# A two-layer decoder trunk on one core: query and gate tiles ahead of the value tiles, an earlier compress, work shared with ScalarE and GpSimd, and a normalisation that needs no second pass

## The reference

```python
h = jnp.einsum('btd,de->bte', x, w_in)          # 1024 -> pool, conv, q, k/v, gates, merge gates
y_a = pool_mixer(pu, ...) * silu(pz)
y_b = cb * short_conv(cc * cx, ...) * silu(cz)
kc = partial_rope(compress(k_cmp_all, ...), kc_end); vc = compress(v_cmp_all, ...)
# attention = g0 * compressed + g1 * selected blocks + g2 * sliding window; gates g = sigmoid(ng)
y_c = nsa_mixer(q, kc, vc, ks, vs, kw, vw, gates, ...) * silu(az)
merged = g_a * (y_a @ proj_a) + g_b * (y_b @ proj_b) + g_c * (y_c @ proj_c)
z = ALPHA * x + merged @ w_out
mu = mean(z); var = mean((z - mu) ** 2)
x = (z - mu) * rsqrt(var + 1e-5) * ln_g + ln_b
```

## Time and profile before

| | us |
|---|---|
| median of 3 runs | 802.36 |
| lowest, highest | 801.02, 804.2 |
| the profiled execution, its own time | 804.0 |
| its span, first to last instruction | 802.3 |
| PE busy | 770.2 (96%) |
| DVE busy | 557.0 (69%) |
| ACT busy | 400.2 (50%) |
| POOL busy | 90.5 (11%) |

### The profile page before, as it was taken

One profiled execution on the slowest core, in us unless ns is written; L12 is line 12 of the kernel. 1 busy time (PEld: TensorE's weight loads), 2 busy tenths in 40 slices (PEclk: granted clock), 3 DMA queues, 4 the chain that ended last, 5 costly groups with the idle time before them and its releaser, 6 DMA issues.

```text
span 802.3 us, 16955 instructions
## 1 busy us (share of the span) xinstructions
PE 770.2 (96%) x6354; PEld 720.4 (90%) x6354; DVE 557.0 (69%) x1038; ACT 400.2 (50%) x793; POOL 90.5 (11%) x166
## 2 busy tenths in 40 slices
PE   8999979999999999999999978799999999999995
PEld 8998778888889999999879978788988999999994
DVE  4564679997679575657465666799886876665664
ACT  5442456666555444443345442676755464444423
POOL 2333430000133100000000034200000000000000
PEclk9999999999999999999999998999999999999998
DMA  8988756533868766555348786636348356665521
GB/s 313 285 272 294 228 179 216 190 103 107 293 227 261 233 179 181 179 181 175 106 136 229 257 246 209 235 113 211 103 123 308 118 183 184 184 183 175 181 93 55
DMA packets 42331, 154.95 MB, mean 193 GB/s; under 512 B 6416, under 2 KB 7440, under 8 KB 41616
## 3 DMA queue, kind: packets, MB, share of 16 engines
q1 hardware_dynamic: 33952, 115.55, 45.8%
q0 software_dynamic: 8304, 38.37, 14.4%
HBM read 145.77 MB, written 13.34 MB: 198 GB/s over the span
## 4 chain that ended last, share of the span: by engine, by line
PE 87%; DVE 6%; DMA 2%; ACT 2%; issue 1%; SPq 0%; DVEq 0%; ACTq 0%
PE bank L664 22%; PE bank L665 22%; PE bank L666 22%; PE bank L682 3%; PE bank L882 3%; DMA ring<-weights_dram 2%; DVE w_lo L1199 2%; PE bank L826 1%; PE bank L832 1%; PE bank L837 1%; PE bank L675 1%; PE bank L1003 1%; PE bank L923 1%; PE bank L1012 1%; PE bank L862 1%
## 5 line engine op out<-in xcount | busy, mean ns | idle before, releaser
L1199 DVE TENSOR_TENSOR w_lo<-ring,w_hi 128x1024 fp32r<-128x1024 f32 x202 | 248.3, 1231 | 155.7 <-ACT w_hi L1021 151.8
L664 PE MATMUL bank<-x_hi,w_hi 128*128 128x264 f32 x1208 | 352.5, 292 | 2.2 <-DVE w_lo L1199 2.2
L666 PE MATMUL bank<-x_lo,w_hi 128*128 128x264 f32 x1208 | 344.5, 285 | 0.0
L665 PE MATMUL bank<-x_hi,w_lo 128*128 128x264 f32 x1208 | 344.4, 285 | 0.0
L1021 ACT ACTIVATE w_hi<-ring 128x1024 fp32r<-128x1024 f32 x202 | 213.3, 1057 | 68.9 <-PE bank L666 34.0
L664 PEld LDWEIGHTS bank<-x_hi,w_hi 128*128 128x128 f32 x1208 | 229.9, 190 | 6.6 <-issue 3.3
L665 PEld LDWEIGHTS bank<-x_hi,w_lo 128*128 128x128 f32 x1208 | 229.9, 190 | 0.4
L666 PEld LDWEIGHTS bank<-x_lo,w_hi 128*128 128x128 f32 x1208 | 228.8, 189 | 0.0
L664 PE MATMUL bank<-h_rounded,w_hi 128*128 128x264 f32 x352 | 102.2, 290 | 0.0
L665 PE MATMUL bank<-h_rounded,w_lo 128*128 128x264 f32 x352 | 100.2, 285 | 0.0
L1073 ACT ACTIVATE h<-bank 128x264 f32<-128x264 f32 x88 | 34.6, 393 | 99.0 <-PE bank L666 90.6
(11 more groups left out here) (253 smaller groups left out, 994.6 us busy)
## 6 DMA issues: line engine op xcount, KB each, us to landing
ring<-weights_dram SPq DMA_DIRECT2D x208, 512.0 KB, 3.7
cache_a<-kcmp_dram POOLq DMA_DIRECT2D x32, 128.0 KB, 3.8
cache_b<-vcmp_dram POOLq DMA_DIRECT2D x32, 128.0 KB, 3.5
cache_a<-ksel_dram POOLq DMA_DIRECT2D x32, 128.0 KB, 4.2
cache_b<-vsel_dram POOLq DMA_DIRECT2D x32, 128.0 KB, 2.6
cache_a<-kwin_dram POOLq DMA_DIRECT2D x2, 2048.0 KB, 11.7
cache_b<-vwin_dram POOLq DMA_DIRECT2D x2, 2048.0 KB, 8.9
kv_dram<-h POOLq DMA_DIRECT2D x2, 1584.0 KB, 6.9
```

The lines of the kernel that those rows point to most:

```text
L664: pe.matmul(out, w_high[:, k0 + k, :], high, start=(k == 0), stop=False)
L665: pe.matmul(out, w_rest[:, k0 + k, :], high, start=False, stop=False)
L666: ins = pe.matmul(out, w_high[:, k0 + k, :], rest, start=False, stop=(k == kn - 1))
L1199: dve.tensor_tensor(w_lo[:, slot % RING], ring[:, slot % RING], w_hi[:, d % HI_RING].bitcast(F32), ALU.subtract).then_inc(w_lo_ready, 1)
```

## The change

The first 25 tiles come in another order (`FIRST_TILES`): the four value tiles VS, VW stand behind Q and NG. The small steps are listed by place (`AFTER_PLACE`), and those of the compress products by layer (`COMPRESS_STEPS`): in layer two cmp_k and cmp_v stand behind places 13 and 14. The row copies of cmp_swap are shared: two larger copies on DVE and two on ACT in place of eight on DVE. q_pad goes from DVE to GpSimd, behind the loads of the selected values. The new rows of k and v are stored by two DMAs in place of one, and k_split waits for that of the keys alone.

The normalisation takes z less a shift (the mean of the channels of tile 0), sums z and its squares while the out tiles run (GpSimd adds tile by tile, ACT squares), and takes the variance as mean of squares less squared mean. Left of the matmuls by ones are five in each layer: one for the shift, two for the mean and two for the squares; the idle matmuls go.

```diff
@@ -91,19 +91,27 @@
...
-AFTER_DENSE = {
-    8: [("rope", 0)], 9: [("cmp_swap", 0)], 10: [("rope", 1), ("cmp_swap", 1)], 13: [("v_rows", 0), ("v_rows", 1)],
-    15: [("v_new_in", 0)], 16: [("rope", 2)], 17: [("cmp_k", 0)], 18: [("v_new", 0), ("rope", 3)], 19: [("cmp_sum", 0)],
-    20: [("rope", 4), ("cmp_rope", 0), ("cmp_v", 0), ("gates", 0)], 21: [("rope", 5), ("q_pad", 0)],
-    22: [("cmp_scores", 0), ("k_split", 0), ("cmp_sum", 1)], 23: [("cmp_vrows", 0), ("cmp_back", 0)],
-    24: [("q_split", 0), ("cmp_soft", 0)]}
+FIRST_TILES = [*range(KC, VS), *range(Q, NG + 1), *range(VS, Q), *range(NG + 1, 25)]
+COMPRESS_STEPS = (
+    {16: [("cmp_k", 0)], 18: [("cmp_sum", 0), ("cmp_v", 0)], 19: [("cmp_rope", 0)], 20: [("cmp_sum", 1)]},
+    {13: [("cmp_k", 0)], 14: [("cmp_v", 0)], 15: [("cmp_sum", 0)], 17: [("cmp_rope", 0)], 19: [("cmp_sum", 1)]})
+AFTER_PLACE = {
+    8: [("rope", 0)], 9: [("cmp_swap", 0)], 10: [("rope", 1)], 11: [("cmp_swap", 1)], 12: [("rope", 2)],
+    14: [("rope", 3)], 16: [("rope", 4)], 17: [("gates", 0)], 18: [("rope", 5)],
+    20: [("cmp_scores", 0)], 21: [("cmp_vrows", 0), ("cmp_back", 0)],
+    22: [("v_rows", 0), ("v_rows", 1), ("v_new_in", 0), ("k_split", 0)], 23: [("cmp_soft", 0), ("v_new", 0)], 24: [("q_split", 0)]}
+
+
+AFTER_OUT = {1: [("shift", 0)], 3: [("square", 0), ("square", 1)], 4: [("square", 2), ("square", 3)],
+             5: [("square", 4)], 6: [("square", 5)]}
...
-    for n in range(25):
-        order += [("dense", n)] + AFTER_DENSE.get(n, [])
+    for n, tile in enumerate(FIRST_TILES):
+        order += [("dense", tile)] + AFTER_PLACE.get(n, [])
+        order += COMPRESS_STEPS[l].get(n, [])
...
-        order.append(("out", i))
-        if i:
-            order.append(("mean", i - 1))
+        order += [("out", i)] + AFTER_OUT.get(i, [])
     if l == DEPTH - 1:
-        return order + [("mean", KT8 - 1), ("warm", 0), ("squares", 0), ("norm", 0)]
-    order += [("pre_k", 0), ("mean", KT8 - 1), ("pre_k", 1), ("pre_k", 2), ("squares", 0)]
-    order += [("pre_k", t) for t in range(3, KT8)] + [("pre_v", t) for t in range(KT8)]
+        return order + [("mean", 0), ("square", 6), ("square", 7), ("norm", 0)]
+    order += [("pre_k", 0), ("mean", 0), ("pre_k", 1), ("square", 6), ("square", 7)]
+    order += [("pre_k", t) for t in range(2, KT8)] + [("pre_v", t) for t in range(KT8)]
...
+                pool.memset(zf[:, 0:NB * GP * 32], 0.0).then_inc(q_pad_clear, 1)
+                pool.wait_ge(q_pad_clear, l + 1)
+                go()
...
+                for i in range(1, KT8 - 1):
+                    if i == 1:
+                        pool.wait_ge(shifted, l + 1)
+                    else:
+                        wait_emptied(pool, l, "out", i)
+                    go()
+                    pool.tensor_tensor(z_sum, z_sum if i > 1 else z[:, 0, :], z[:, i, :], ALU.add).then_inc(z_summed, 1)
+                    pool.wait_ge(squared, l * KT8 + i + 1)
+                    go()
+                    pool.tensor_tensor(h[:, 0, :], h[:, 0, :], h[:, i, :], ALU.add).then_inc(squares_summed, 1)
+                    pool.wait_ge(z_summed, l * (KT8 - 2) + i)
+                    pool.wait_ge(squares_summed, l * (KT8 - 2) + i)
...
+                    elif step == "shift":
+                        wait_emptied(pe, l, "out", 0)
+                        pe.matmul(bank[SA][:, 0:T], ones[:, :], z[:, 0, :], start=True, stop=True).then_inc(shift_sum, 1)
+                    elif step == "square":
+                        if i == KT8 - 2:
+                            pe.wait_ge(squares_summed, (l + 1) * (KT8 - 2))
+                            pe.matmul(bank[SB][:, 0:T], ones[:, :], h[:, 0, :], start=True, stop=False)
+                        elif i == KT8 - 1:
+                            pe.wait_ge(squared, (l + 1) * KT8)
+                            pe.matmul(bank[SB][:, 0:T], ones[:, :], h[:, i, :], start=False, stop=True
+                                      ).then_inc(squared_sum, 1)
...
                     elif step == "mean":
...
+                        pe.wait_ge(shift_ready, l + 1)
+                        pe.wait_ge(z_summed, l * (KT8 - 2) + KT8 - 2)
+                        pe.matmul(bank[SA][:, 0:T], ones[:, :], z_sum, start=True, stop=False)
+                        wait_emptied(pe, l, "out", KT8 - 1)
+                        pe.matmul(bank[SA][:, 0:T], ones[:, :], z[:, KT8 - 1, :], start=False, stop=True
+                                  ).then_inc(mean_ready, 1)
...
+                    elif step == "cmp_swap":
+                        own = (cache_a, cache_b)[i][:, CMP_CACHED:CMP_CACHED + CMP_OWN].rearrange(
+                            "p (s u g c) -> p u g c s", u=2, g=4, c=CT)
+                        act.wait_ge(own_landed[i], (l + 1) * 2 * 16)
+                        for j in range(2):
+                            rows = slice(j * HD, j * HD + HD)
+                            ins = act.activation(own[rows, 0, 1 - j::2, :, :], z[rows, 4 + 2 * i:6 + 2 * i, 0:SEQ].rearrange(
+                                "p g (c j s) -> p j g c s", c=CT, j=2)[:, j], ACT.Copy)
+                        ins.then_inc(cmp_swapped, 1)
...
+                    elif step == "shift":
+                        act.wait_ge(shift_sum, l + 1)
+                        act.activation(z_shift, bank[SA][:, 0:T], ACT.Copy, scale=float(KT8)).then_inc(shift_ready, 1)
+                    elif step == "square":
+                        if i < 2:
+                            act.wait_ge(shifted, l + 1)
+                        else:
+                            wait_emptied(act, l, "out", i)
+                        act.activation(h[:, i, :], z[:, i, :], ACT.Square).then_inc(squared, 1)
                     elif step == "norm":
-                        for k in range(4):
-                            act.wait_ge(centered, l * 4 + k + 1)
-                            act.activation(m[:, 2 * k:2 * k + 2, :], z[:, 2 * k:2 * k + 2, :], ACT.Square
-                                           ).then_inc(squared, 1)
-                        act.wait_ge(squared_sum, l + 1)
-                        act.activation(rstd[:, :], bank[SB][:, 0:T], ACT.Sqrt, bias=eps[:, :]).then_inc(std_ready, 1)
+                        act.wait_ge(mean_ready, l + 1)
+                        act.activation(mean_sq, bank[SA][:, 0:T], ACT.Square).then_inc(mean_squared, 1)
+                        act.wait_ge(var_ready, l + 1)
+                        act.activation(rstd[:, :], rstd[:, :], ACT.Sqrt, bias=eps[:, :]).then_inc(std_ready, 1)
...
+                    if step == "gates":
                         wait_emptied(dve, l, "dense", NG)
...
+                        for n in range(2):
+                            wait_emptied(dve, l, "dense", (KC, VC)[i] + n)
+                        for j in range(2):
+                            rows = slice(j * HD, j * HD + HD)
+                            dve.tensor_copy(own[rows, 0, j::2, :, :], h[rows, (KC, VC)[i]:(KC, VC)[i] + 2, 0:SEQ].rearrange(
+                                "p g (c j s) -> p j g c s", c=CT, j=2)[:, j])
...
-                        dve.wait_ge(kv_stored, (l + 1) * 16)
+                        dve.wait_ge(k_stored, (l + 1) * 16)
...
-                        wait_slot(dve, l, step, i)
-                        emptied_by(dve.scalar_tensor_tensor(out=z[:, i, :], in0=z[:, i, :], scalar=ALPHA,
-                                                            in1=bank[FILL[l, step, i, 0][0]][:, 0:T],
-                                                            op0=ALU.mult, op1=ALU.add), step, i)
+                        if i == 2:
+                            dve.wait_ge(shift_ready, l + 1)
+                            dve.tensor_tensor(z[:, 0:2, :], z[:, 0:2, :], z_shift.unsqueeze(1).to_broadcast([P, 2, T]),
+                                              ALU.subtract).then_inc(shifted, 1)
...
+                        psum = bank[FILL[l, step, i, 0][0]][:, 0:T]
+                        if i < 2:
+                            wait_slot(dve, l, step, i)
+                            emptied_by(dve.scalar_tensor_tensor(out=z[:, i, :], in0=z[:, i, :], scalar=ALPHA, in1=psum,
+                                                                op0=ALU.mult, op1=ALU.add), step, i)
+                        else:
+                            link(dve.scalar_tensor_tensor(out=z[:, i, :], in0=z[:, i, :], scalar=ALPHA, in1=z_shift,
+                                                          op0=ALU.mult, op1=ALU.subtract))
+                            wait_slot(dve, l, step, i)
+                            emptied_by(dve.tensor_tensor(z[:, i, :], z[:, i, :], psum, ALU.add), step, i)
...
                     elif step == "norm":
-                        dve.wait_ge(mean_ready, l + 1)
-                        wait_emptied(dve, l, "out", KT8 - 1)
-                        wait_emptied(dve, l, "out", KT8 - 2)
+                        dve.wait_ge(mean_squared, l + 1)
                         for k in range(4):
```

(10 more changed lines are left out.)

93 lines of the change are left out of this document (38 added, 55 removed).

## The result

The changed kernel takes 796.14 us (median of five, 794.87 to 800.28), the kernel before 803.3 on the same chip: a ratio of 0.9923, 95% interval 0.9903 to 0.9944. The forecast was 786.0 with a range from 780.5, so the time lies 2 us above its upper end; 7.2 us were saved where 16.4 were forecast. The profiled execution is the slowest of the five (800.28, span 798.6); its trace shows about 4 us more than a usual execution has.

What follows compares the result with a forecast made beforehand. PE, busy 96%, bounds the kernel with its own work and its waits. First stages 5.1, clock 3.4, normalisation 9.2, less 0.5 and 0.8, give 16.4 us: 786.0 us against the median 802.36, range 780.5 to 794.

Steps and rivals of the forecast that it cites:

- The wait before the scores: First stage of each layer: PE still waits for q_split, about 4.0 us (3.0 to 4.8) where 3.1 stood.
- The tail: End of layer two: last z tile to reciprocal takes 5.2 us, before 7.2; gain 2.0.
- The terms 4.95 + 2.25 + 2.0: Normalisation gains: fewer matmuls by ones in layer one, in layer two, and a shorter end; together 9.2 us.
- The padding on GpSimd: Moved q_pad falls into the scores, where turns wait for DVE: costs 0.4 us per layer, 0 to 1.
- it is requested when tile 13 ends (time 0): Layer two's place-16 weight: PE needs 15.2 us to the gate matmul, DVE 17.3 from request; wait 2.1 (1.5 to 3.0).
- R3: Rival: close compress slots in layer two make weights 3 us late and the clock falls again; 792.4 us, chance 0.10.
- its 3.4 us goes too: Clock in layer two: without the group of three waits, the loss behind them goes; gain 3.4 us (0 to 6.8).
- R4: Rival: waits move without being removed and half the normalisation's gain is lost; 4 us gain, 798.4 us, chance 0.04.
- I take 0.6: Normalisation: each GpSimd add of 264 columns takes 0.6 us; DVE's cycle per out tile becomes 3.6 against 2.9.
- just what splitting two tiles ahead lends: Out stage: DVE's lag of 0.7 us a tile over four tiles, 2.8, is covered, so PE isn't stopped.
- The charge: Cost of GpSimd's adds: 0.5 us for a later end in layer one, bounds 0 and 5.6.
- R2: Rival: DVE's lag reaches PE in the out stage, 2.8 us per layer, q_pad costs 1 each; 792.3 us, chance 0.13.

Runs made afterwards that it cites:

- e16: Kernel combining four follow-up edits (775.70 us: layer two's compress moved, q_split and v_new early, residual sums early, gate product early), with the gate product late again: 779.00 us.
- e14: The kernel combining four follow-up edits (775.70 us), with the old normalisation put back, its residual sums early as well: 784.57 us.
- e15: The kernel combining four follow-up edits (775.70 us), with layer two's compress steps back at places 13, 14, 15, 17 and 19: 783.35 us.
- e2: Changed kernel with the old normalisation put back, so new order, shared copies and padding on GpSimd alone: 802.33 us, ratio 0.9989 to the kernel before.
- e17: The kernel combining four follow-up edits (775.70 us), with the residual sums of x_hi and x_lo back in the out stage: 779.15 us.
- e7: Changed kernel with GpSimd's normalisation adds cut from 264 to 8 columns, leaving out most of both sums: 794.33 us.

## Why the prediction was wrong

**Right.** The wait before the scores stayed at 3.7 in each layer (4.0 predicted), released by q_split; the 3.7 for the turned values and layer one's 1.2 went; layer one's gate wait is 0.3 (0.5), the wait for the bank of the gates 0.6 (0.7). The tail is 5.1 (5.2). The late gate product by itself costs a wait of 2.2 in e16 (2.1), but there the compress stands elsewhere, so the nearness proves little. The terms 4.95 + 2.25 + 2.0 of the normalisation were 9.1 together in e14 (9.2). The padding on GpSimd shows nowhere (no run has it alone): the turn's 2.5 us are 2.5.

**First failed step: "it is requested when tile 13 ends (time 0). From there PE needs ... DVE can begin at 5.2".** The sum counted VectorE's work from the moment a weight is asked for, and took the asking as punctual. It isn't: two slots of 1.8 us close together empty the ring faster than it fills, ACT waits for a weight with the last tile's copy behind it, SP's swap waits for that copy, and further loads wait behind the swap. Of this the rival R3 had the first half (the slots and the crossings in SP's queue), with 3 us and a chance of 0.10; its objection, that loads are five slots ahead, counted the slots' number and not how short two of them are. The chain through ACT's queue was in no rival. By e15 the close places, chain and clock included, cost 8.1 us, against an expected gain of 2.5 there (5.3 of old waits less 2.8).

**Second: "With the group of three waits in layer two gone as a group, its 3.4 us goes too".** The group came back as four waits and took more clock (5.1 lost in the trace). In e2 the waits of the whole program are 22.9 us, 22.8 before: the order moved them and removed none, which was R4's first half (0.04).

**Third, a size: "I take 0.6 ... So PE isn't stopped, and I charge 0.5".** The adds take 1.1 to 1.2 us in the mean, and two of VectorE's operations stretch by 0.55 and 0.45 beside them. VectorE's cycle is 3.54 us for a tile of 2.91. The prediction had 3.6, near it by luck: the adds are nearly twice as long, but hold VectorE up for 1.0 us a tile and not for their whole length. The step that failed is the cover, "just what splitting two tiles ahead lends". PE doesn't wait for a split there; it waits for a bank that VectorE's last z operation empties (L1676), three times in a layer, and the lead of the splits doesn't cover that. The charge was 3.9 us (e17), inside its own bounds of 0 to 5.6, so the first half of R2 (0.13) was the true mechanism, at 3.9 and not its 5.6. The prediction cited the Trainium skill, "SBUF — State Buffer", section "SBUF: two separate sides", for a port pair held by one of the two engines; the trace agrees, with operations on two SBUF inputs at 0.67 to 0.98 (0.43 beside e7's short adds) and the one that reads PSUM at 0.43. It can also be the add that is held up: beside the split at 376.15, which keeps its 1.22, an add takes 1.75 (at 376.24).

In the sum, on the trace: 16.4, less 5.0 for more waits in layer two (7.8 for 2.8), less 5.1 + 1.6 for the clock there and behind the scores (3.4 to be won, 1.7 and 1.6 lost), less 3.4 for the adds (the 3.9 of e17 for 0.5), and 0.8 + 0.6 back for the padding and the shorter waits before the scores, is 2.7; the two profiled executions differ by 804.0 - 800.3 = 3.7. By the medians it is 7.2, since the usual execution of the changed kernel is 4 us better than the profiled one: e2, with the same order and about the same waits (22.9 us in all, against 25.8 less the out stages' 2.7), lost 5.1 us to the clock in its trace where the changed kernel lost 10.1. The losses to the clock are counted in full here, though part of them falls into waits. R2 and R3 came true at once; the range treated them as alternatives, and so did not hold their sum.

## What to carry to other kernels

A ring that is five loads ahead is only as deep as the time of its slots: before two short products are put side by side, add up in time, not in slots, and look at what stands behind the engine's wait for a load in the same queue (here a copy that the DMA queue itself needed). Cost an engine's cycle in a stage with the stretched durations beside GpSimd, and if it comes out over PE's, move an operation to a stage with room rather than hope for the lead. When several waits are each below what a run can tell, build the kernel without all of them and undo one at a time: prices of 4 us, hidden before in other waits and in the clock, could be told there. And a short wait of TensorE costs more than the idle time in the trace (0.63 for 0.39 here): count from start to start.
